# A hybrid encoder step: the sample's group of the recurrence first, attention's rest beside the group norm, and a unit's scores in front of the preceding unit's transposes

## The reference, cut to what matters

```python
# RWKV-7: 4 heads of 64, a matrix state per head, then group norm, bonus and gate
def step(Sm, inp):
    sa = einsum('bhij,bhj->bhi', Sm, kk_t)
    Sm = Sm * w_t - sa[..., None] * (kk_t * a_t) + v_t[..., None] * k_t
    return Sm, einsum('bhij,bhj->bhi', Sm, r_t)
y = (y - mean) * rsqrt(var + GN_EPS) * gn_w + gn_b      # per head of 64
y = (y + bonus) * g
# latent attention: 8 heads; prompt block-causal in blocks of 128, sample over 256 past + 32 own keys
s = (q_lat @ ckv + q_rope @ kr) * MLA_SCALE
o = softmax(s) @ ckv
```

## Time and profile before

| | |
|---|---|
| time, median of 3 runs | 2092.05 us (2091.1 to 2097.66) |
| profiled execution | 2097.62 us, its span 2095.8 us |
| PE busy | 1927.3 us (92%) |
| DVE, ACT, POOL busy | 991.0, 721.2, 95.8 us |
| mean granted TensorE clock | 0.953 of 2.4 GHz |
| DMA | 149.51 MB, 71 GB/s mean |

### The profile page before, as it was taken

The page is one execution under the profiler, slowest core; times in us unless marked ns, Lnnn a source line. Parts: engine busy times, 40 slices in busy tenths (PEclk is TensorE's granted clock), DMA queues, the critical chain, the costliest instruction groups (busy, mean ns, idle before and its releaser), DMA issues.

```text
span 2095.8 us, 37479 instructions
## 1 busy us (share of the span) xinstructions
PE 1927.3 (92%) x16506; PEld 1750.6 (84%) x16506; DVE 991.0 (47%) x1695; ACT 721.2 (34%) x1272; POOL 95.8 (5%) x100
## 2 busy tenths in 40 slices
PE   6977999899879999999999599998998899999997
PEld 6955777699759999999999366768986799999997
DVE  6565544354334544444364755525532355353533
ACT  4263444444234222222232544433523342221212
POOL 2000000210001000000100000001000100000001
PEclk9988998699999999999999699978999899999998
DMA  5200000255102222222221000003520122222221
GB/s 211 91 7 1 2 2 3 77 183 181 47 21 71 93 92 89 91 81 91 90 82 61 7 2 2 2 3 141 175 99 29 51 81 91 91 81 91 86 86 63
DMA packets 38593, 149.51 MB, mean 71 GB/s; under 512 B 4384, under 2 KB 4544, under 8 KB 36768
## 3 DMA queue, kind: packets, MB, share of 16 engines
q1 hardware_dynamic: 36288, 131.05, 18.3%
q0 software_dynamic: 2144, 16.06, 2.0%
HBM read 139.68 MB, written 7.41 MB: 70 GB/s over the span
## 4 chain that ended last, share of the span: by engine, by line
PE 86%; DVE 7%; ACT 4%; issue 1%; POOL 0%; DMA 0%; DVEq 0%; ACTq 0%; SPq 0%; POOLq 0%
PE PS L484 76%; PE PS L595 8%; PE PS L807 1%; PE PS L901 1%; DVE stat L1608 1%; DVE mP L1617 1%; DVE wL L1307 1%; DVE rs L1601 1%; DVE aq L1600 1%; DVE aq L1603 1%; DVE aP L1617 1%; ACT hH L932 1%; POOL sq L420 0%; ACT wH L932 0%; ACT ell L932 0%
## 5 line engine op out<-in xcount | busy, mean ns | idle before, releaser
L484 PE MATMUL PS<-hH,wH 128*128 128x272 f32 x2272 | 485.3, 295 | 35.9 <-DMA cst<-cst_in 15.8
L484 PE MATMUL PS<-hH,wL 128*128 128x272 f32 x2272 | 475.8, 291 | 0.0
L484 PE MATMUL PS<-hL,wH 128*128 128x272 f32 x2272 | 475.7, 291 | 0.0
L1307 DVE TENSOR_TENSOR wL<-ring,wH 128x1024 fp32r<-128x1024 f32 x238 | 301.0, 1266 | 221.5 <-ACT wH L932 221.1
L484 PEld LDWEIGHTS PS<-hH,wH 128*128 128x128 f32 x2272 | 359.8, 190 | 47.1 <-DMA cst<-cst_in 15.8
L932 ACT ACTIVATE wH<-ring 128x1024 fp32r<-128x1024 f32 x238 | 249.7, 1051 | 356.0 <-PE PS L484 356.0
L484 PEld LDWEIGHTS PS<-hH,wL 128*128 128x128 f32 x2272 | 361.8, 190 | 0.0
L484 PEld LDWEIGHTS PS<-hL,wH 128*128 128x128 f32 x2272 | 359.9, 191 | 0.0
L484 PE MATMUL PS<-hidH,wL 128*128 128x272 f32 x1024 | 212.0, 288 | 0.0
L484 PE MATMUL PS<-hidH,wH 128*128 128x272 f32 x1024 | 211.7, 288 | 0.0
L484 PE MATMUL PS<-hidL,wH 128*128 128x272 f32 x1024 | 211.1, 288 | 0.0
(11 more groups left out here) (275 smaller groups left out, 2540.1 us busy)
## 6 DMA issues: line engine op xcount, KB each, us to landing
ring<-wall SPq DMA_DIRECT2D x238, 512.0 KB, 3.3
lw<-lw_in POOLq DMA_DIRECT2D x2, 2240.0 KB, 9.0
xT<-x_in SPq DMA_DIRECT2D x4, 544.0 KB, 6.2
y_out<-hT SPq DMA_DIRECT2D x8, 272.0 KB, 2.1
mem<-mem_in POOLq DMA_DIRECT2D x2, 1024.0 KB, 5.1
mks<-mks_in POOLq DMA_DIRECT2D x2, 1024.0 KB, 9.2
mvs<-mvs_in POOLq DMA_DIRECT2D x2, 1024.0 KB, 11.8
memk_out<-mkp POOLq DMA_DIRECT2D x2, 1024.0 KB, 5.4
```

The lines of the kernel that those rows point to most:

```text
L484: return e.matmul(out, lhsT=a, rhs=b, start=start, stop=stop)
L1307: tt(wL[:, n % SPLIT], ring[:, n % RING], plain(wH[:, n % SPLIT]), ALU.subtract).then_inc(w_lo, 1)
```

## The change

1. Lane 0 becomes groups 0, 2; lane 1 becomes 4, 1, 3 (`LANES`, `lane_of`). Lane 1 is 17 steps longer: its first 14 (group 4 up to its last `merge`) run alone behind the factor slots, then 36 pairs alternate, and the last 3 (blocks and states of group 3) end it.
2. The order is a written string of turns, "r" for the recurrence and "a" for attention: two attention steps after each of the four factor slots, one or two in turn after each of the 14 lone steps, one after every second step of the pairs, then three after each of four steps of the group norm, and five at the end.
3. `group_norm` is the end of the recurrence's program, so its steps stand between attention steps; DVE's and ACT's splits of the first output tiles are its fourth step.
4. In a unit, `score(u)` comes before `turn(u-1)` on PE, and ACT's exp(u) before `turned_out(u-1)`; `weigh` and `head_out` follow one unit later (u-2).
5. S has a third slot for the sample's final state; POOL stores it as soon as group 4 is through, and the prompt's at the end.

```diff
+LANES = [list(range(0, NG - 1, 2)), [NG - 1] + list(range(1, NG - 1, 2))]
+def lane_of(g):
+    return int(g in LANES[1])
 def _rec_steps():
-    slots = [[("factor", 0, i)] for i in range(4)]
-    lanes[1][:0] = [None] * 3
-    for i in range(max(map(len, lanes))):
-        slots += [[lane[i]] for lane in lanes if i < len(lane) and lane[i]]
-    return slots
+    alone = len(lanes[1]) - len(lanes[0]) - 3
+    lanes[1], first = lanes[1][alone:], lanes[1][:alone]
+    slots = [("factor", 0, i) for i in range(4)] + first
+    for pair in zip(*lanes):
+        slots += pair
+    return slots + lanes[1][-3:], 4 + alone
+def _turns():
+    order = ""
+    for i in range(len(REC_STEPS)):
+        order += "r"
+        if i < 4:
+            order += "aa"
+        elif i < ALONE:
+            order += "a" * (1 + i % 2)
+        elif i % 2 == ALONE % 2:
+            order += "a"
+    for i in range(NORM_STEPS):
+        order += "raaa"
+    return order + "a" * (ATT_STEPS - order.count("a"))
 def weave(recurrence, attention):
-    done = 0
-    for i, _ in enumerate(recurrence):
-        upto = (i + 1) * ATT_STEPS // len(REC_SLOTS)
-        for _ in range(upto - done):
-            next(attention, None)
-        done = upto
-    for _ in attention:
-        pass
-+    for turn in TURNS:
+        next(recurrence if turn == "r" else attention, None)
+    for program in (recurrence, attention):
+        for _ in program:
+            pass
 # PE, a unit of attention
+                        score(u)
                         if u:
                             turn(u - 1)
-                        score(u)
                         yield
                         if h + 1 < HEADS:
                             project(5 * (h + 1) + b)
-                        if u:
-                            weigh(u - 1)
+                        if u >= 2:
+                            weigh(u - 2)
 # POOL
-                e.wait_ge(s["state_out"], at(l, "state_out", NCH - 1))
+                e.wait_ge(s["state_out"], at(l, "state_out", nth("state", NG - 1)))
+                put("wkv", outs["wkv_out"][l, :, 1], S[:, 2, :, :])
+                e.wait_ge(s["state_out"], at(l, "state_out", NCH))
                 put("wkv", outs["wkv_out"][l, :, 0], S[:, 0, :, :])
 # PE, ACT and DVE, in each recurrence(): behind its last step
+                    yield from group_norm()
                 weave(recurrence(), attention())
-                in_turn(group_norm())
```

More of the change, by code:

```diff
@@ L118, in chunks_of @@
     return (0, 1) if g < NG - 1 else (0,)
+LANES = [list(range(0, NG - 1, 2)), [NG - 1] + list(range(1, NG - 1, 2))]
+def lane_of(g):
+    return int(g in LANES[1])
 def _rec_steps():
[L123 to L129, removed]
-    slots = [[("factor", 0, i)] for i in range(4)]
-    lanes[1][:0] = [None] * 3
-    for i in range(max(map(len, lanes))):
-        slots += [[lane[i]] for lane in lanes if i < len(lane) and lane[i]]
-    return slots
+    lanes = []
+    for groups in LANES:
+        lane = []
+        for g in groups:
+            lane += [("tokens", g, 0), ("score_l", g, 0), ("score_m", g, 0), ("merge", g, 0)]
+            for b in range(1, LEVELS):
+                lane += [("cross", g, b), ("merge", g, b)]
+            lane += [("solve", g, 0), ("blocks", g, 0)] + [("state", g, c) for c in chunks_of(g)]
+        lanes.append(lane)
+    alone = len(lanes[1]) - len(lanes[0]) - 3
[4 more added lines that the diff above has]
+    return slots + lanes[1][-3:], 4 + alone
 LEVELS = 6
-REC_SLOTS = _rec_steps()
-REC_STEPS = [step for slot in REC_SLOTS for step in slot]
+REC_STEPS, ALONE = _rec_steps()
 ATT_STEPS = 3 + 2 * len(UNITS) + 1
+NORM_STEPS = 4
+def _turns():
[11 more added lines that the diff above has]
+    return order + "a" * (ATT_STEPS - order.count("a"))
+TURNS = _turns()
 PER_LAYER = {
@@ L227, in build @@
         ctx0 = carve(col["end"], MIX, **one, TK=(3, 256), BK=(2, 256))
-        S, = carve(col["end"], MIX, S=(2, 2, CH))
+        S, = carve(col["end"], MIX, S=(3, 2, CH))
         assert col["S"] >= col["rh"] + 2 * T
@@ L343, in weave @@
         def weave(recurrence, attention):
[L345 to L352 removed]
+            for turn in TURNS:
+                next(recurrence if turn == "r" else attention, None)
+            for program in (recurrence, attention):
+                for _ in program:
+                    pass
         def two_banks(x, a, b, rows=slice(0, 128)):
@@ L729, in recurrence @@
                 def recurrence():
[L730 to L747, removed]
+                    for kind, g, b in REC_STEPS:
+                        if kind == "tokens":
+                            tokens(g)
+                        elif kind == "score_l":
+                            score_l(g)
+                        elif kind == "score_m":
+                            score_m(g)
+                        elif kind == "cross":
+                            cross(g, b)
+                        elif kind == "merge":
+                            merge(g, b)
+                        elif kind == "solve":
+                            solve(g)
+                        elif kind == "blocks":
+                            blocks(g)
+                        elif kind == "state":
+                            state(g, b)
                         yield
+                    yield from group_norm()
                 def group_norm():
@@ L1076, in recurrence @@
                 def recurrence():
[L1077 to L1086, removed]
+                    for kind, g, b in REC_STEPS:
+                        if kind == "factor" and b == 2:
+                            decays()
+                        elif kind == "tokens":
+                            tokens_out(g)
+                        elif kind == "merge":
+                            merged_out(g, b)
+                        elif kind == "solve":
+                            solved_out(g)
                         yield
+                    yield from group_norm()
                 def group_norm():
@@ L1161, in attention @@
                             (nope_out if b < 3 else keys_out)(5 * (h + 1) + b)
-                        if u:
-                            head_out(u - 1)
+                        if u >= 2:
+                            head_out(u - 2)
                         yield
                     turned_out(len(UNITS) - 1)
+                    head_out(len(UNITS) - 2)
                     yield
@@ L1550, in recurrence @@
                 def recurrence():
[L1551 to L1566, removed]
+                    for kind, g, b in REC_STEPS:
+                        if kind == "factor":
+                            (decay_sums if b < 2 else factors)(b)
+                        elif kind == "score_l":
+                            score_l_out(g)
+                        elif kind == "score_m":
+                            score_m_out(g)
+                        elif kind == "cross":
+                            cross_out(g, b)
+                        elif kind == "solve":
+                            diagonals(g)
+                        elif kind == "blocks":
+                            blocks_out(g)
+                        elif kind == "state":
+                            states_out(g, b)
                         yield
+                    yield from group_norm()
                 def group_norm():
```

59 lines of the change are left out of this document (30 added, 29 removed).

## The result

The changed kernel took 2062.95 us (median of 4 runs, 2059.62 to 2064.88) against 2094.29 for the kernel before on the same chip: a ratio of 0.985, 95% interval 0.983 to 0.987, 31 us less. The profiled execution has a span of 2060.7 us instead of 2095.8.

A forecast was written before the change was run, and what follows sets the result against it. PE was taken as bound by its number of matmuls, plus holes, low clock and a lone norm. Output projection at 350 + 41 = 391 instead of 400.6 saves 9.6 us, 19 over both layers: 2092.05 - 19 = 2073; range 2048 to 2098.

The forecast's parts named there:

- Factor slots: Start of the woven stretch: longer by 11.2 us per layer, first `tokens` at 178.8 against 167.63.
- five attention steps in return: In the factor slots: five more attention steps done there, about 5 us of full-clock PE work.
- Last `state`: End of the recurrence's groups, before the norm: at 350 us, against 378 before.
- I take 8 us of holes in all: PE's idle time between first `tokens` and last `state`: 8 us, ends 3 and 15.
- 4.1 for the low clock: After the first `tokens`: some 10 us at half the clock, costing 4.1 us.
- 159 of work: PE's full-clock work left up to the last `state`: 159 us.
- rival D: Factor slots cost more, or waits before the transposes stay behind the query piece: 3 us per layer each, 2085; chance 0.12.
- the prices of the prediction: PE's cost in the woven stretch: about 1.13 us per attention step, 1.03 us per recurrence step.
- The factor 1.7 for half the clock: PE steps at 1.2 GHz: assumed to take about 1.7 times as long as at full clock.
- Tail: From last `state` to output projection, norm beside attention: 41 us, ends 33 and 50.
- Rival A: Group 4's matmuls hold the clock low throughout its lone stretch: 22 us per layer, 2117, slower; chance 0.13.
- threshold of 24 us: Low clock beyond some 24 us after the first `tokens`: the low-clock case decides, from 10 us per layer.

The follow-up runs named there:

- short_factor: Changed kernel with three attention steps in the factor slots instead of eight, the other five in group 4's lone stretch: 2055.43 us, ratio 0.976 to 0.982.
- s_only: Kernel before with only the order inside a unit changed (scores first, weighted values one unit later): 2063.72 us, ratio 0.981 to 0.989.
- s_only_b: Kernel before with only the order inside a unit changed, run again in more rounds on another chip: 2058.35 us, ratio 0.981 to 0.987.
- no_s: Changed kernel with the old order inside a unit put back: 2102.91 us, ratio 1.003 to 1.007 to the kernel before.
- no_n: Changed kernel with the group norm alone behind everything and attention spread evenly: 2068.65 us, ratio 0.984 to 0.990 to the kernel before.
- l_only: Kernel before with only the group order changed, group 4 first: 2085.81 us, ratio 0.993 to 0.997.
- dense_lone: Changed kernel with the norm alone, three attention steps in the factor slots, 21 in group 4's lone stretch, the rest even: 2060.58 us.
- L: The part of the change that puts group 4 first; alone against the kernel before: 2085.81 us.
- S: The part of the change that reorders the inside of a unit; alone against the kernel before: 2063.72 and 2058.35 us.
- N: The part that puts the norm beside attention's rest, with its turns; changed kernel without it: 2068.65 us.
- no_lag: Kernel before with scores ahead of the transposes, but weighted values not delayed by a unit: 2097.78 us, ratio 0.998 to 1.002.
- no_l: Changed kernel with the old lanes, group 4 alone at the end, 67 attention steps spread evenly: 2081.80 us, ratio 0.992 to 0.996 to the kernel before.
- dense_end: Kernel before with the new order inside a unit and attention denser at the end (22 steps over the last 14 slots): 2057.01 us, ratio 0.978 to 0.983.

## Why the prediction was right, and where it was not

The direction and the range were right, 19 us forecast and 31 measured. Step by step, in layer 0 from the start of the scans (they began 1.7 us earlier than before):

- Factor slots: first `tokens` forecast 30.8 us after the scans, measured 176.73 - 146.22 = 30.5. L1512 and `decays` came within 0.3 us of where they were put. This step was read rightly, in-order queues and all. I booked it with five attention steps in return; short_factor shows the account was negative by some 5 us in the layer where the clock held, a single layer of a single trace.
- Last `state`: forecast 350, less those 1.7, 348.3; measured 336.0. The step that failed is "I take 8 us of holes in all", with 4.1 for the low clock and 159 of work. Measured: holes 2.1 us, low clock 5.3 us long (2.2 lost), work 5.3 / 1.7 + 43.3 + 108.6 (the 109.2 of the third window less its part behind 336.0) = 155.0. The holes are the largest miss: 12.2 us before (1.6, 9.6 and 1.0 in the three windows of the earlier trace rows), of which I let 4 go where 10 went. My fear that `normalise` behind the query piece keeps the wait (rival D) was unfounded: what hides it is a score, a projection and a recurrence step, about 3 us by the prices of the prediction, against a chain of 2.7. The factor 1.7 for half the clock came out: 30.09 us of PE against 17.49 for the 206 matmuls of s_only and s_only_b.
- Tail: forecast 41, measured 379.5 - 336.0 = 43.5. The norm's work on ACT and DVE did stall attention, at the two places named (2.9 us before unit 34's projection, 2.6 after the splits), and the full clock lasted to 350 only.
- Rival A (the low clock stays beside group 4) did not happen in the changed kernel, but it is real: no_s, no_n, l_only, and later dense_lone and short_factor show it, for 21 to 40 us. Its threshold of 24 us after the first `tokens` was summed wrongly: 4.1 booked and 10 more lost are 14.1 us, and with 0.41 lost per us at the low clock (1 - 1 / 1.7) that is 34 us. no_n, with the low clock until some 31 us after the first `tokens`, lies within it and is faster than before; l_only, with 41 us in layer 1, is faster too, as it no longer has the 33 us at 0.52 at the end. The rule of the Trainium skill ("TensorE: Matmul & The Clock Gate", Part 1), a clock that follows how busy PE is, is again not what the rows show: 39.41 of 40 us busy at 0.53.

The right range came from a sum whose largest term was near, but put down to a cause that it did not need. For a layer my sum had 13.5 us of clock won back (17.6 lost before, 4.1 after) and 4.2 us of holes, less 1.8 in the tail and 6.2 in the factor slots: 9.7. In layer 0 of the trace these are, by the same reckoning, 15.4 and 10.1, less 0.3 and 5.8: 19.4. I put the clock down to group 4 leaving the end, and the experiments show that it can be had without: the order inside a unit by itself gives as much as the whole change (30 and 38 us), in part through the clock, and the rest of the change gives nothing on top that can be told from noise: 2063.7 and 2058.4 without, 2063.0 and 2064.1 with. That the range held with the holes at less than half their worth, and with a cause that was not needed, is in part luck.

The parts do not add. L is worth 10 us without S; with S it is worth nothing that shows (2068.7 in no_n and 2060.6 in dense_lone, against 2063.7 and 2058.4). N costs 18 to 23 us with S and the old lanes; with the new ones (no_n against the changed kernel) it is 5 us to the good, within overlapping ranges.

Left open: what holds the clock up. It does not follow PE's busy share, nor the density of attention alone (0.9 steps per step held at the end in s_only_b, and 1.9 fell in layer 1 of short_factor). Fewer holes do not do it alone either: no_lag, with 4.7 us of holes instead of 11.2 up to group 3's last `state` in layer 0, has the clock of the kernel before (0.949 to 0.958), as has no_l (0.951 to 0.953). All I can say from these traces is that it fell in or near the stretches where one group is alone, and behind the last projections, and that S as a whole had it higher than the kernel before in nearly every execution.

## What to carry to other kernels

- When PE's waits are short and many, look at what stands directly behind the awaited result in PE's own queue: putting independent work (the next scores) ahead of the waiting instruction, and letting its consumer lag one unit, left 1.3 us of 10.3 in layer 0. The lag is needed: without it part of the wait moves to the next copy, and nothing is gained. The lag without the new order was not run.
- Do not take PE's busy time for work done. Count the matmuls, or look when a given instruction ends: in no_lag PE was busy 5.7 us more in 156 us with not one matmul more.
- Before moving work beside a serial epilogue, price it there and where it is: attention beside the norm cost 1.4 us a step in the tail, against 1.13 in the pairs.
- Put a bundled change apart before crediting it. Here one of three parts by itself gave as much as all three, and two versions, one with less change and one with two lines altered, have the lower medians: dense_end and short_factor, 2057.0 and 2055.4 us against 2064.1. They ran on another chip than the bundle; their ratios to the kernel before, at most 0.983 and 0.982, lie at or below the bundle's 0.983 to 0.987.
- Where an execution's clock is on record, compare kernels at an equal clock too: it tells a change's own worth from the clock's (18 us of the 30 to 38 for S, none for no_lag).

## What the runs showed of the hardware that was not expected

- The same kernel (s_only_b) took 2054.1 to 2075.1 us on one chip, and the times go by the mean granted clock, 0.969 to 0.955. Two traces of it, on two chips, show where: 0.53 against 1.00 over the matmuls of group 4's end, 11 us in layer 0.
- The clock can stay at 1.2 GHz while PE is busy all the time: 39.41 of 40 us in short_factor, 30.09 of 30.2 in s_only.
- A step of 8 matmuls of 64x64 takes PE as long as one of 16 (0.68 us each); at half the clock it takes 1.11 us, 1.6 times as long, not twice.
